# Seven products in place of eight for part of the last down projection of a two-layer trunk

## What is computed

```
def conv_ffn(h, w_up, conv_w, conv_b, w_down):
    u = causal_depthwise_conv(h @ w_up, conv_w, conv_b)
    val, gate = jnp.split(u, 2, axis=-1)
    return (jax.nn.gelu(gate) * val) @ w_down
...
x = x + conv_ffn(...)          # layer 1: (256 x 5632) @ (5632 x 2048)
```

## Time and profile before

| | us |
|---|---|
| median of 3 runs | 2274.09 |
| lowest, highest | 2272.08, 2274.53 |
| span of the profiled execution | 2272.6 |
| TensorE matmuls busy | 2264.1 |
| VectorE busy | 1502.4 |
| ScalarE busy | 1268.4 |
| GpSimd busy | 619.1 |

### The profile page before, as it was taken

The page is one execution under the profiler, slowest core; times in us unless marked ns, Lnnn a source line. Parts: engine busy times, 40 slices in busy tenths (PEclk is TensorE's granted clock), DMA queues, the critical chain, the costliest instruction groups (busy, mean ns, idle before and its releaser), DMA issues.

```text
span 2272.6 us, 33897 instructions
## 1 busy us (share of the span) xinstructions
PE 2264.1 (100%) x11072; PEld 1911.0 (84%) x11072; DVE 1502.4 (66%) x1812; ACT 1268.4 (56%) x1663; POOL 619.1 (27%) x1027
## 2 busy tenths in 40 slices
PE   9999999999999999999999999999999999999999
PEld 7888888988888888888888888898888888888887
DVE  6766775676767667665556778658767767665443
ACT  6655664565556555544444777556655655554333
POOL 0720001234343343412221100215434344340000
PEclk9999999999999999999999999999999999999999
DMA  8655435547776776766665555636867676776555
GB/s 274 207 199 200 133 126 176 176 151 219 217 223 214 222 222 213 222 206 202 203 203 188 174 193 175 200 126 216 253 220 221 216 223 212 221 221 193 194 193 167
DMA packets 143779, 455.24 MB, mean 200 GB/s; under 512 B 25888, under 2 KB 26784, under 8 KB 143696
## 3 DMA queue, kind: packets, MB, share of 16 engines
q1 hardware_dynamic: 117696, 420.40, 58.0%
q0 software_dynamic: 25856, 33.65, 4.9%
q10 hardware_dynamic: 144, 0.06, 0.0%
HBM read 423.73 MB, written 2.10 MB: 187 GB/s over the span
## 4 chain that ended last, share of the span: by engine, by line
PE 99%; ACT 0%; DVE 0%; DMA 0%; issue 0%; SPq 0%; ACTq 0%
PE ps L412 50%; PE ps L417 25%; PE ps L370 10%; PE ps L374 5%; PE ps L355 2%; PE ps L391 2%; PE ps L729 1%; PE ps L978 1%; PE ps L715 0%; PE ps L809 0%; PE ps L698 0%; PE ps L637 0%; DMA xT<-in_x_t 0%; PE ps L691 0%; PE ps L830 0%
## 5 line engine op out<-in xcount | busy, mean ns | idle before, releaser
L343 DVE TENSOR_TENSOR w_lo<-raw,w_hi 128x1024 fp32r<-128x1024 f32 x788 | 978.8, 1245 | 702.4 <-ACT w_hi L337 699.6
L337 ACT ACTIVATE w_hi<-raw 128x1024 fp32r<-128x1024 f32 x787 | 830.8, 1059 | 855.7 <-PE ps L417 738.7
L412 PE MATMUL ps<-w_hi,xg_hl 128*128 128x512 f32 (+1 forms) x3392 | 832.9, 388 | 1.9 <-DVE xg_hl L1462 1.9
L412 PEld LDWEIGHTS ps<-w_hi,xg_hl 128*128 128x128 f32 x3392 | 631.8, 188 | 131.4 <-DVE xg_hl L1462 2.4
L417 PE MATMUL ps<-w_lo,xg_hl 128*128 128x512 f32 (+1 forms) x1696 | 450.1, 388 | 0.0
L412 PE MATMUL ps<-w_hi,a_hl 128*128 128x512 f32 x1656 | 411.9, 391 | 0.3 <-ACT vmem L1110 0.2
L417 PEld LDWEIGHTS ps<-w_lo,xg_hl 128*128 128x128 f32 x1696 | 317.0, 188 | 65.3
L412 PEld LDWEIGHTS ps<-w_hi,a_hl 128*128 128x128 f32 x1656 | 308.8, 188 | 65.0 <-issue 0.7
L2140 POOL DMA_DIRECT2D u_t<-z_t x704 | 346.5, 500 | 2.8 <-issue 2.8
L417 PE MATMUL ps<-w_lo,a_hl 128*128 128x512 f32 x828 | 221.4, 389 | 0.0
L417 PEld LDWEIGHTS ps<-w_lo,a_hl 128*128 128x128 f32 x828 | 155.4, 188 | 32.5
(11 more groups left out here) (215 smaller groups left out, 1779.2 us busy)
## 6 DMA issues: line engine op xcount, KB each, us to landing
raw<-in_w_stream SPq DMA_DIRECT2D x787, 512.0 KB, 4.2
u_t<-z_t POOLq DMA_DIRECT2D x704, 34.0 KB, 3.4
bias<-in_rel_bias POOLq DMA_DIRECT2D x4, 768.0 KB, 5.8
memT<-in_mem_t POOLq DMA_DIRECT2D x4, 512.0 KB, 6.0
gate_w<-in_gate_w POOLq DMA_DIRECT2D x4, 512.0 KB, 3.8
x_tok<-x_turned SPq DMA_DIRECT2D x16, 128.0 KB, 4.3
out_t<-x_tok SPq DMA_DIRECT2D x8, 256.0 KB, 4.3
u_dn<-z_dn POOLq DMA_DIRECT2D x48, 32.0 KB, 3.2
```

What stands on the lines that cost most here:

```text
L337: nc.scalar.activation(w_hi[:, s, :], raw[:, s, :], ACT.Copy).then_inc(hi_done, 1)
L343: nc.vector.tensor_tensor(w_lo[:, s, :], raw[:, s, :], w_hi[:, s, :].bitcast(F), ALU.subtract).then_inc(lo_done, 1)
L412: nc.tensor.matmul(ps[:, bank + tt, 0:n], a[:, k0 + k, tt * P:tt * P + P], w_hi[:, s, k * n:k * n + n], start=start and k == 0 and q == 0, ...
```

## The change

Take a pair of K-tiles k = 1, 2, the token tiles 1, 2 and a pair of column tiles 1, 2. Before, their product is eight products of 128x128 by 128x512. Winograd's form of Strassen's scheme does it by seven, of sums of the activation blocks and sums of the weight blocks, with sums of the results.

Six of the 22 pairs (u = 0 to 5, `PAIRED`) are done this way, for each of the two pairs of column tiles (q = 0, 1): twelve paired steps, n = 0 to 11. `LAST_ORDER` gives the new order: for q = 0 five ordinary pairs (u = 6 to 10), then a paired step ("s") and two ordinary pairs ("c") in turn; for q = 1 two ordinary pairs and then the same. An ordinary pair is now two units, one for each column tile of the pair, into banks 0, 1 and 2, 3. The host orders the stream accordingly.

A paired step has four splits in place of two: the whole of its first unit, the second half of its second unit ("h"), and two tiles of weight sums ("t"), each of them 1024 columns. TensorE does 6, 3, 6 and 6 matmuls on them, into banks 0 to 2 and 4 to 7 (`paired`).

The weight sums: SP loads two half units into `t_in` (`sums_first`), two steps ahead; GpSimd adds a third half unit to both by two transfers with `accum_op=ADD`; VectorE makes two more sums of 512 columns from it and `raw` into `t_raw` (`weight_sums`), ahead of the step's first low half. Of the second unit SP now loads only the second half.

The activation sums (`forms`, for two of the six pairs at a time, b = 0, 1, 2): GpSimd adds high and low halves again (1024 columns) and makes four sums of 256 columns; this section stands behind `halos(1)` in GpSimd's list, and each group stands ahead of the adding transfers of its step. ScalarE and VectorE split the sums, 1024 columns each, after the split at position 6, 14 and 22 (`FORMS_AT`), behind `value_slot` of the same position. TensorE waits for this (`form_lo`) at the start of steps 0, 2 and 4.

The results of the seven products gather in banks 4 to 7 besides 0 and 2. After the sixth step of a q, ScalarE copies bank 4 to `u_sum`, and VectorE makes seven operations (`product_sums`, in three parts before three successive low halves), six of 512 columns and one of 1024, all into `x_tok` or `u_sum`. The adds of banks 0, 1 and 2, 3 come with them (`tile_adds`). TensorE waits for these adds before the next q's first units (`tile_done`) and for the sums before its first step (`sum_done`).

```diff
+PAIRED = 6
+LAST_ORDER = [[("c", u) for u in range(6, 11)] + [x for j in range(5) for x in (("s", j), ("c", 11 + 2 * j), ("c", 12 + 2 * j))] + [("s", 5), ("c", 21)],
+              [("c", 6), ("c", 7)] + [x for j in range(PAIRED) for x in (("s", j), ("c", 8 + 2 * j), ("c", 9 + 2 * j))] + [("c", 20), ("c", 21)]]
+FORMS_AT = {6: 0, 14: 1, 22: 2}
...
+        def last_lo(dve, e):
...
+            dve.wait_ge(hi_done, e + 1)
+            nc.vector.tensor_tensor(w_lo[:, s, cols], src, w_hi[:, s, cols].bitcast(F), ALU.subtract).then_inc(lo_done, 1)
...
+            def sums_first(n):
+
+                c, z = RAW_OF[n], n % 2
+                if n >= 2:
+                    sp.wait_ge(lo_done, WSUM_SPLIT[n - 2, 0] + 1)
+                    sp.wait_ge(wsum_ready, 2 * (n - 2) + 1)
+                sp.dma_start(t_in[:, z, 0:COLS], t["w_stream"][c, :, 0:COLS]).then_inc(t_loaded[z], 16)
+                sp.dma_start(t_in[:, z, COLS:UE], t["w_stream"][c + 1, :, COLS:UE]).then_inc(t_loaded[z], 16)
...
+                for n, c0 in RAW_OF.items():
+                    if old in (c0, c0 + 1):
+                        sp.wait_ge(wsum_ready, 2 * n + 2)
+                    if c == c0 + 6 and n + 2 in RAW_OF:
+                        sums_first(n + 2)
...
+                def paired(u, e, n):
...
+                    if j % 2 == 0:
+                        pe.wait_ge(form_lo, min(n // 2, PAIRED // 2 - 1) + 1)
+                    if j == 0:
+                        if n:
+                            pe.wait_ge(sum_done, 1)
+                        else:
+                            pe.wait_ge(up_out, TT * 4 * UP_ITER)
+                    work = (((first_cols, a_part(0, 0), 4), (second_cols, a_part(1, 0), 0)),
+                            ((second_cols, s_part(3), 2),),
+                            ((first_cols, s_part(0), 5), (second_cols, s_part(2), 7)),
+                            ((first_cols, s_part(1), 6), (second_cols, a_part(1, 1), 1)))
...
+            def weight_sums(n):
...
+                dve.wait_ge(t_added[z], 32 * (n // 2 + 1))
+                V.tensor_tensor(t2, t1, b22, ALU.add).then_inc(wsum_ready, 1)
+                dve.wait_ge(wsum_ready, 2 * n + 1)
+                V.tensor_tensor(t4, t2, b21, ALU.add).then_inc(wsum_ready, 1)
...
+            def product_sums(q, part):
...
+                if part == 0:
+                    dve.wait_ge(p1_out, q + 1)
+                    ch.link(dve, V.tensor_tensor(x_tok[:, n0, 0, :], x_tok[:, n0, 0, :], u_sum[:, :], ALU.add))
+                    ch.link(dve, V.tensor_tensor(u_sum[:, :], u_sum[:, :], ps[:, 6, :], ALU.add))
+                    ch.link(dve, V.tensor_tensor(x_tok[:, n1, 0, :], x_tok[:, n1, 0, :], u_sum[:, :], ALU.subtract))
...
+                for e in range(c0 + SLOTS, END + SLOTS):
+                    pos = e - SLOTS - c0
+                    if e in SUMS_AT:
+                        q, part = SUMS_AT[e]
+                        dve.wait_ge(pe_unit, WSUM_SPLIT[PAIRED * (q + 1) - 1, 1] + 1)
+                        product_sums(q, part)
+                    if e in ADDS_AT and ADDS_AT[e][0] < 3:
+                        n, done = ADDS_AT[e]
+                        dve.wait_ge(pe_unit, done + 1)
+                        tile_adds(n)
+                    if e in SUM_BEFORE:
+                        weight_sums(SUM_BEFORE[e])
+                    if e < END:
+                        last_lo(dve, e)
+                    if pos < 9:
+                        value_slot(1, UP_ITER, pos)
+                    if pos in FORMS_AT:
+                        b = FORMS_AT[pos]
+                        dve.wait_ge(form_hi, b + 1)
...
+            def forms(b):
...
+                ch.link(pool, G.tensor_tensor(a_f[:, 4 * b:4 * b + 4, :, 0, :],
...
+                ch.link(pool, G.tensor_tensor(s1, a21, a22, ALU.subtract))
+                ch.link(pool, G.tensor_tensor(s2, s1, a11, ALU.subtract))
+                G.tensor_tensor(s3, a11, a21, ALU.subtract)
+                G.tensor_tensor(s4, a12, s2, ALU.add).then_inc(form_made, 1)
+
+            def last_section():
+                for n, c in RAW_OF.items():
+                    if n < PAIRED // 2:
+                        forms(n)
+                    z = n % 2
+                    pool.wait_ge(t_loaded[z], 32 * (n // 2 + 1))
+                    for h in range(2):
+                        pool.dma_start(t_in[:, z, h * COLS:(h + 1) * COLS], t["w_stream"][c + 1, :, 0:COLS],
+                                       accum_op=ALU.add).then_inc(t_added[z], 16)
...
             halos(1)
+            last_section()
```

More of the change, by code:

```diff
@@ L145, in trunk @@
         rb = at("rb", top[0], [TT, P])
+        u_sum = at("u_sum", top[0], [COLS])
         sq = sb("sq", [SEQ])
@@ L269, in trunk @@
         out_done = sem("out_done")
+        form_made, form_hi, form_lo = sem("form_made"), sem("form_hi"), sem("form_lo")
+        t_loaded = [sem(f"t_loaded{s}") for s in range(2)]
+        t_added = [sem(f"t_added{s}") for s in range(2)]
+        wsum_ready, p1_out, sum_done = sem("wsum_ready"), sem("p1_out"), sem("sum_done")
         chains = {n: Chain(sem(f"{n}_self")) for n in ("act", "dve", "pool")}
@@ L545, in _ @@
                                  x_turned[SQ * b:SQ * b + SQ, a, :, :, :].rearrange("p t k j -> p (t k j)")).then_inc(x_tok_in, 16)
-            units(x_moved + 3 * SLOTS, N_UNITS)
+            units(x_moved + 3 * SLOTS, first["down1"])
+            def sums_first(n):
[5 more added lines that the diff above has]
+                sp.dma_start(t_in[:, z, COLS:UE], t["w_stream"][c + 1, :, COLS:UE]).then_inc(t_loaded[z], 16)
+            for n in range(2):
+                sums_first(n)
+            for c in range(first["down1"], N_UNITS):
+                old = c - SLOTS
+                sp.wait_ge(lo_done, SPLIT_OF.get(old, old) + 1)
+                for n, c0 in RAW_OF.items():
[3 more added lines that the diff above has]
+                        sums_first(n + 2)
+                if c - 1 in RAW_OF.values():
+                    sp.dma_start(raw[:, c % SLOTS, COLS:UE], t["w_stream"][c, :, COLS:UE]).then_inc(raw_full[c % SLOTS], 16)
+                else:
+                    unit(c % SLOTS, c)
             for n in range(4):
@@ L908, in value_there @@
                         pe.wait_ge(g_lo, UP_ITER + k // 4 + 1)
[L910 to L919, removed]
@@ L921, in last_section, with product @@
-                c = N_UNITS - 1
+                def product(e, cols, form, bank, start, stop, done):
+                    x_hi, x_lo = form
+                    s = e % SLOTS
+                    if done is None:
+                        for q, x in enumerate((x_hi, x_lo)):
+                            nc.tensor.matmul(ps[:, bank, :], x, w_hi[:, s, cols], start=start and q == 0, stop=False)
+                        return None
+                    return nc.tensor.matmul(ps[:, bank, :], x_hi, w_lo[:, s, cols], start=False, stop=stop)
@@ new lines, in last_section @@
+                pe.wait_ge(proj_free, fblock["down1"] + 2)
+                for q, kind, u, e, n in LAST:
+                    if kind == "s":
+                        paired(u, e, n)
+                        continue
+                    begin, end = u == PAIRED, u == TOK_DOWN - 1
+                    for b in range(2):
+                        if q and b and end:
+                            continue
+                        token_unit(pe, e + b, 2 * u, 2, a_hi, a_lo, 2 * b, begin, end, value_there if q == 0 and b == 0 else None,
+                                   (lambda tt, b=b: pe.wait_ge(tile_done, 2 * b + tt + 1)) if q and begin else None)
@@ L922, in last_section @@
+                c = END - 1
                 s, k0 = c % SLOTS, FT - 2
@@ L2241, in _stream @@
         down = by_squares(down) if l else np.concatenate([in_runs(down[:, :3 * COLS]), down[:, 3 * COLS:]], 1)
-        parts += [blocks(down, 2, COLS)]
+        down = blocks(down, 2, COLS)
+        if l:
+            down = down[[TOK_DOWN * (2 * q + b) + u for q in range(2) for _, u in LAST_ORDER[q] for b in range(2)]]
+        parts += [down]
     return np.ascontiguousarray(np.concatenate(parts, 0))
```

119 lines of the change are left out of this document (104 added, 15 removed).

## The result

The changed kernel takes 2284.15 us (median of 7 runs, 2282.61 to 2286.78), the kernel before 2273.41 (7 runs on the same chip). The ratio is 1.0045, with a 95% interval of 1.0035 to 1.0055: slower by some 10 us. The profiled execution took 2284.15 us, with a span of 2282.5; the prediction had 2280.9 for the span and 2282.4 for the time.

The account below looks back on a forecast made before the run. TensorE was taken as the bound, busy 2264.1 of 2272.6 us. On that span, -8.2 (matmuls) + 12.8 (first step) + 3.4 (pair change) + 0.3 (tail) gave 2280.9, so a time of 2282.4 us; range 2273.5 to 2289.

Parts of the forecast that it names:

- The removal: Twelve paired steps of 21 matmuls in place of 24: 36 fewer, 8.16 us of TensorE, all on the path.
- The steady step, at nothing: Later paired steps cost nothing: VectorE 10.6 and ScalarE 8.0 us within TensorE's 15.64; transfer cover about 10 us.
- rival (c): Adding transfers slow in kind: landing above some 13 us is paid ten times, 15 us give about 2300; chance 0.05.
- The first step: Step 0 ends 12.8 us late (3.0 to 14), as VectorE and GpSimd wait for each other's whole instruction.
- the walk: Step 0's queues followed by the earlier trace's clock: TensorE starts 11 us late, the step ends at 2074.7, not 2061.9.
- the clock: Lower granted clock after step 0's gap: nothing taken, up to 1.5 us, as the step waits for low half 12 anyway.
- The change of column pair: After step 5 TensorE waits for VectorE's sums and adds: 3.4 us, 2.6 without gaps; clock up to 1.6, none taken.
- The tail: At the kernel's end, two more output transfers within the last 3 us: 0.3 us taken, 0 to 1.
- The sum: Whole kernel: 2272.6 - 8.2 + 12.8 + 3.4 + 0.3 = 2280.9 us span, 2282.4 us time.
- Rival (d): Both gaps, step 0 and pair change, bring the lower clock unhidden: 2282.4 + 3 = 2285.5; chance 0.05.
- (a): It cancels: VectorE and GpSimd disturb one another little and adds land soon, 2271.8, some 2277 with half the contention; chance 0.24.
- (b): Faster: first forms and adds are there before TensorE reaches step 0, only the pair change is paid, 2268.8; chance 0.06.

Follow-up runs that it names:

- e8_groups_later: Changed kernel with GpSimd's second and third group of forms made only after steps 0 and 1, steps spaced to units 6, 20, 28; 2280.27 us.
- e3_forms_vector: Changed kernel with VectorE making the activation sums itself, in two parts, and GpSimd only issuing the adding transfers; 2273.81 us, ratio 1.0015 to the kernel before.
- e2_forms_writes: Changed kernel with GpSimd's additions replaced by memsets that keep it about as long at work but read nothing; 2278.48 us.
- e6_both: e3_forms_vector with VectorE's `x_tok` additions of banks 0 to 3 put ahead of `product_sums` at the pair change; 2271.21 us, ratio 0.9993 to the kernel before.
- e7_loads_first: e6_both with the plain loads for two steps ahead issued behind the next step's raw loads; 2269.72 us, ratio 0.9983 to the kernel before.
- e9_adds_apart: e7_loads_first with step 1's adding transfers held back until those of step 0 have landed; 2267.69 us, ratio 0.9979 to the kernel before.

## Why the prediction was right, and where its terms were off

**The removal** (-8.16): right, 36 matmuls less in the trace.

**The steady step, at nothing**: right. There is no wait in steps 1 to 5, with the transfer share at 0.85 against the 0.75 to 0.9 forecast. The landing in the steady part was 6.9 us and not 5, and well inside the cover of 10; rival (c) had no ground.

**The first step** (+12.8): the mechanism and the releaser (the forms' low half) as forecast, the size 16.85. Two terms were mis-sized. First the walk: TensorE started 14.44 late in place of 11. GpSimd's last halo copy, from the start of the section, came 1.5 us later than in the kernel before (at 17.4 and 15.9 us), and its new work with it. The walk gave the convolution 5.6 us, with only small operations of GpSimd between, and e8_groups_later, where that is so, has 5.18; it took 10.35, as the second group's large addition fell into it whole, and the third group's fell into a sum of 512 columns (4.05). Against that, 3.5 us of waiting for the transfers, which the walk had (landing at 2059.0), did not occur; the landing itself, 4.5 us, was near the 4.8 taken. The 7.1 us that the convolution took longer are about the length of the GpSimd operations beside it (3.02, and six of 0.8); the walk had too few of them meet. Second the clock: "nothing taken, up to 1.5" was wrong. Step 0 was expected to stand waiting for low half 12 in any case, but VectorE, freed of GpSimd, was ahead again, and TensorE was busy for all 7.17 us:

```profile
2068.80 2.07 PE L1001 MATMUL ps<-w_hi,a_hl 128*128 128x512 f32 x4 [14.28 <-DVE s_hl L2077]
...
2074.61 0.61 PE L1001 MATMUL ps<-w_hi,s_hl 128*128 128x512 f32 x2
```

Four matmuls in 2.07 us there, two in 0.61 at the end of the step: 2.41 us for the clock.

**The change of column pair** (+3.4): 3.94 measured, but in other parts. The first wait was 2.0, as worked out (2.1). The second (1.1) did not come, as the unit before it ran at the low clock and gave VectorE the time (the adds ended at 2165.78, TensorE came at 2166.22); in e3_forms_vector, at full clock there, a second wait of 0.52 did come. The clock, "none taken, as TensorE is busy right before and after", cost 1.8. Two errors of nearly the same size met here.

**The tail** (+0.3): nothing can be seen of it; from the end of the last matmul to the end of the span it is 3.2 us in both kernels. The prediction put the second pair's sums under the last four units; eight follow the last step, so the cover was twice as large.

**The sum.** With the right terms the sum on the span of before is 2285.2; the 2.78 us that the changed kernel's execution gained at its start made it 2282.5. The forecast of 2280.9 was thus nearer than its terms were, which was luck: they were 4.4 us too little in the section. Rival (d), low clock at both gaps, is what happened, on top of the forecast's own mechanism and with 4.2 us for the two where it had 3. Rivals (a) and (b), that the engines disturb one another little or that the forms are there in time, fall with the rows above.

## What to carry to other kernels

A saving of matmuls spread evenly over a section (here 8.16 us) is easily lost at its two ends, where the new work must first be ready and last be cleared away: look there for the engine that is nearly full already, and put no two-input work of GpSimd beside it. VectorE did GpSimd's five additions in 3 us of its own, and with the transfers of the first step issued alone and the adds that free the banks ahead of the sums, the same idea gained 5 us instead of losing 10. A first wait tells only part of a price when TensorE is the bound; ask at what clock it goes on.

## What the runs showed of the hardware

- GpSimd's writes leave VectorE alone (e2_forms_writes: convolution 3.48, forms' low half 1.22 us), and so does its issuing of transfers (e3_forms_vector: 3.25); its two-input reads don't (10.35 and 3.44). The Trainium skill (GPSIMD Engine Reference, Specifications) calls the SBUF interfaces shared with VectorE where VectorE has two SBUF inputs; the trace agrees. It shows besides that what GpSimd does counts as well, and that beside two inputs of GpSimd an instruction of VectorE waits for the whole one of GpSimd: a low half that began 0.05 us behind GpSimd's 2.40 us ended 3.44 us after its start, 1.1 us behind GpSimd's end.
- The same wait of TensorE doesn't always bring the same clock. At the change of the pair 1.96 us of waiting was followed by 3.26 us for eight matmuls in the changed kernel, and 1.95 us by 2.16 in e3_forms_vector:

```profile
2149.29 2.16 PE L473 MATMUL ps<-w_hi,a_hl 128*128 128x512 f32 x8 [1.95 <-DVE x_tok L2024]
```

- In step 0 short waits between small groups of matmuls were followed by a granted clock of 0.50 in e6_both and e7_loads_first, and by none in e3_forms_vector and e9_adds_apart. The first of these waits was 1.44 and 1.40 us in the two that fell, 0.81 and 0.36 in the two that didn't; the others were 0.2 to 0.9 in all four. Whether the first wait decides it, these four traces don't show. The price was 1.3 and 2.3 us.
- Of four adding transfers issued together the first two had landed 8.1 us after the first issue (e7_loads_first, 2046.74 to 2054.86), two alone after 5.9 (e9_adds_apart, 2047.91 to 2053.82); VectorE's wait fell from 4.7 to 2.4 us.
- Two executions differed by 2.8 us in their first 12 us, and kept the difference for 2000 us. A change of a few microseconds is best read from the length of its own section, beside medians of many executions.
